# A joint between two layers: the sums of squares of the first half stand between the last down products, the other half's norm sum behind the first mixer tiles

## The reference

```python
# end of the first block
h = rmsnorm(x, g_ffn_pre) * (1 + scale_f) + shift_f
f = (silu(h @ w_gate) * (h @ w_up)) @ w_down
x = x + gate_f * rmsnorm(f, g_ffn_post)
# start of the second block
h = rmsnorm_2(x, norm_mix_w)
u = h @ w_in                     # the mixer's wide projection: z, xbc, dt and others
```

## Time and profile before

| | us |
|---|---|
| three runs: median (lowest to highest) | 1715.58 (1715.3 to 1716.63) |
| profiled execution: whole time | 1714.21 |
| profiled execution: span | 1712.4 |
| TensorE busy, share of the span | 1689.9, 99% |
| VectorE, ScalarE, GpSimd busy | 740.5, 715.5, 784.5 |

### The profile page before, as it was taken

How to read it: one execution, slowest core, us unless ns; L and a number is a source line. 1 busy time by engine, 2 the same in 40 slices (tenths; PEclk the granted TensorE clock), 3 DMA queues, 4 the chain that set the end, 5 groups by cost and what they waited for, 6 DMA issues and landing times.

```text
span 1712.4 us, 22126 instructions
## 1 busy us (share of the span) xinstructions
PE 1689.9 (99%) x8068; PEld 1373.4 (80%) x8068; DVE 740.5 (43%) x1142; ACT 715.5 (42%) x967; POOL 784.5 (46%) x612
## 2 busy tenths in 40 slices
PE   7999999999999999999999999999999999999998
PEld 5777798888888888888888888887888788888887
DVE  7767653111110046567678778675104222222002
ACT  5756454222233345334434636544223534433232
POOL 3432244444456654443443434345444444444663
PEclk9999999999999999999999999999999999999999
DMA  8655223233223323432333333223243322222332
GB/s 298 221 180 173 87 87 99 86 98 88 96 68 100 92 68 143 137 99 87 111 99 99 100 98 111 86 85 98 89 140 94 99 90 93 87 97 72 95 92 73
DMA packets 55300, 184.61 MB, mean 108 GB/s; under 512 B 5920, under 2 KB 8224, under 8 KB 54720
## 3 DMA queue, kind: packets, MB, share of 16 engines
q1 hardware_dynamic: 55232, 183.67, 33.6%
HBM read 179.39 MB, written 4.26 MB: 107 GB/s over the span
## 4 chain that ended last, share of the span: by engine, by line
PE 94%; issue 2%; DVE 2%; POOL 1%; DMA 1%; ACT 0%; SPq 0%; DVEq 0%; POOLq 0%
PE PR L560 27%; PE PR L561 26%; PE PR L564 26%; PE AX L1058 1%; PE PR L575 1%; PE PR L576 1%; PE PR L574 1%; PE AX L781 1%; PE AX L807 1%; POOL wlo L500 1%; PE AX L1062 1%; PE AX L791 1%; DMA raw<-w 1%; PE AX L597 1%; PE AX L795 1%
## 5 line engine op out<-in xcount | busy, mean ns | idle before, releaser
L500 POOL TENSOR_TENSOR wlo<-raw,whi 128x512 fp32r<-128x512 f32 (+1 forms) x600 | 778.3, 1322 | 876.4 <-ACT whi L1186 876.4
L1186 ACT ACTIVATE whi<-raw 128x1024 fp32r<-128x1024 f32 x288 | 301.5, 1051 | 141.1 <-PE PR L564 132.4
L560 PE MATMUL PR<-h3h,whi 128*128 128x512 f32 x608 | 245.5, 404 | 0.0
L561 PE MATMUL PR<-h3l,whi 128*128 128x512 f32 x608 | 240.3, 395 | 0.0
L564 PE MATMUL PR<-h3h,wlo 128*128 128x512 f32 x608 | 154.1, 395 | 0.0
L560 PE MATMUL PR<-h4h,whi 128*128 128x512 f32 x351 | 139.4, 397 | 0.0
L561 PE MATMUL PR<-h4l,whi 128*128 128x512 f32 x351 | 138.6, 395 | 0.0
L564 PEld LDWEIGHTS PR<-h3h,wlo 128*128 128x128 f32 x608 | 114.2, 188 | 27.6
L560 PEld LDWEIGHTS PR<-h3h,whi 128*128 128x128 f32 x608 | 114.3, 188 | 26.7 <-issue 1.2
L561 PEld LDWEIGHTS PR<-h3l,whi 128*128 128x128 f32 x608 | 114.4, 188 | 26.4 <-issue 1.0
L560 PE MATMUL PR<-h2h,whi 128*128 128x512 f32 x320 | 126.8, 396 | 0.1
(11 more groups left out here) (375 smaller groups left out, 2972.0 us busy)
## 6 DMA issues: line engine op xcount, KB each, us to landing
raw<-w SPq DMA_DIRECT2D x224, 512.0 KB, 3.5
cond<-wcond SPq DMA_DIRECT2D x48, 512.0 KB, 4.5
raw<-w SPq DMA_DIRECT2D x32, 384.0 KB, 3.1
raw<-w SPq DMA_DIRECT2D x32, 320.0 KB, 2.9
abc_a<-acum_rows SPq DMA_DIRECT2D x8, 512.0 KB, 4.0
abc_b<-acum_rows SPq DMA_DIRECT2D x8, 512.0 KB, 4.3
x<-xin SPq DMA_DIRECT2D x2, 1024.0 KB, 7.1
x_keep<-x SPq DMA_DIRECT2D x1, 2048.0 KB, 8.1
```

The source lines that it names most:

```text
L500: ins = pool.tensor_tensor(wlo[:, j, a:a + n], raw[:, j, a:a + n], whi[:, j, a:a + n], ALU.subtract)
L560: pe.matmul(bank, whi[:, j, w], oh[:, k0 + k, :], start=first and i == 0, stop=False)
L561: pe.matmul(bank, whi[:, j, w], ol[:, k0 + k, :], start=False, stop=False)
L1186: act.activation(whi[:, j, :], raw[:, j, :], ACT.Copy).then_inc(hi_ready, 1)
```

## The change

The sums of the squares of x for the first half (`x_sum(2)`) no longer stand behind all 44 strips. They are placed between the strips of the second half of the last down tile: after the strip given by (unit j, block k) those tiles are added that `SUMS_DN1` names, the last four before the last strip. `mix_sum(3)`, the norm sum of the down projection for the second half, goes from its place in front of the mixer into `first_units`, behind tiles 0 and 1 of the first half and ahead of the wait for tile 2. A wait for the last copy of the down results is added at the head of `first_units`. Only TensorE's list changes; ScalarE, VectorE, GpSimd and SyncE keep theirs.

```diff
+SUMS_DN1 = {(2, 1): (0,), (2, 3): (1,), (3, 1): (2,), (3, 2): (3,), (3, 3): (4, 5, 6, 7)}
...
                         mm = strip(j, fh1, fl1, k0, k, PR[:, 1 + e, :], c, j == 0 and k == 0, j == 3 and k == nk - 1)
+                        if e == 1 and (j, k) in SUMS_DN1:
+                            x_sum(2, SUMS_DN1[j, k])
                     if e == 1:
                         mm.then_inc(unit_used, 1)
                 if e == 0:
                     mm.then_inc(half_done, 1)
-            x_sum(2)
-            mix_sum(3, V_DN1 + N_DN)
...
             def first_units():
 
                 pe.wait_ge(dt_v, 1)
+                pe.wait_ge(mix_ready, R0 + N_OUT + N_DN)
                 for e, c in enumerate(HALF):
                     for k in range(KT):
+                        if e == 0 and k == 2:
+                            mix_sum(3, V_DN1 + N_DN)
                         pe.wait_ge(hh_ready, KT + KT * (2 + e) + k + 1)
```

## The result

| | before | after |
|---|---|---|
| median of nine runs (lowest to highest), us | 1715.58 (1714.54 to 1716.63) | 1719.49 (1717.25 to 1722.59) |
| ratio, 95% interval | | 1.0025 (1.0016 to 1.0033) |
| profiled execution, span | 1712.4 | 1717.7 |
| joint: first strip of the last down tile to first full-width mixer unit | 51.62 | 56.37 |

A forecast was written before the change was run, and what follows sets the result against it. TensorE, busy 99% of the span, was taken as the bound. Terms of 0.56 (first tile), 0.43 (moved sum), 1.52 (second stall), 0.15 and 0.45, taken as 3.2 on 1715.58, gave 1718.8 us; range 1716.4 to 1721.2.

The forecast's parts named there:

- One wait of 1.7 us: TensorE's wait between the last down tile's sums and the first normalised mixer tile: the change's whole target, 0.1% of the kernel.
- Sums between the strips: Last down tile on TensorE: eight moved sums cost 0.43 us each as before and find their squares ready, 0.9 to spare.
- The last down piece comes late: ScalarE ahead of the first half's Ln: square and copy of that piece come later, delaying the first mixer tile by 0.56 us.
- The other half's sum: Behind mixer tile 1: the moved norm sum adds 0.43 us, and tile 2 waits for its Ln and Exp, a 1.5 us stall.
- The two shortfalls: Tile 5's low product from GpSimd, 0.1 to 0.2 us late, and the other half's squares in the second eight sums, +0.45 us.
- Sum +3.2: Whole kernel: the added terms come to 3.1 to 3.2 us, taken as 3.2, +0.19%.
- The clock: Rival: TensorE falls to 1.2 GHz in the first stall, costing 1.6 us, +4.8 in all, 1720.4 us; chance 0.12.
- My row against it: Profile row from 30.76 to 32.24: TensorE idle for 1.48 us while its granted clock stayed at 1.00.
- likeliest case: Whole kernel: forecast of +2.5 to +3.8 us, chance 0.72, with +3.2 just inside the measurable 0.2% (3.4 us).
- The added wait: Head of the mixer's first units: waiting for the copies of all nine down pieces was to cost nothing.

The follow-up runs named there:

- e5: Changed kernel with e1's order, first half's Ln and Exp ahead of the last down piece, sums ended three strips before the tile's end: joint 51.29 us, ratio 0.9998.
- e1: Changed kernel with ScalarE's copies of tiles 2 and 3 put ahead of the other half's Ln and Exp: joint 52.68 us, ratio 1.0013.
- e2: Changed kernel with the other half's norm sum back in front of the mixer: joint 52.16 us, ratio 1.0012.
- e4: Changed kernel with the first stall filled by ten matmuls whose result nobody uses: joint 54.89 us, ratio 1.0019.
- e1b: e1 run and profiled a second time, same code on the changed kernel: joint 53.96 us, ratio 1.0009.
- a2: Changed kernel, unaltered, profiled a third time, one execution only: joint 56.36 us.
- e3: Kernel before with only the norm sum moved behind the first two mixer tiles, plus the added wait: joint 55.87 us, ratio 1.0020.
- c1: Kernel before with only the added wait for the last down piece's copy: joint 51.59 us, median 0.17 us below before.
- e6: Changed kernel with e1's ScalarE order and e4's filling of the first stall: joint 52.69 us, ratio 1.0010.
- e2b: e2 profiled a second time, same code on the changed kernel, one execution only: joint 53.67 us.
- c0: Kernel before, unaltered, timed against itself and profiled again: joint 51.68 us, median 0.65 us below before.

## Why the prediction was right, and where it was not

- **One wait of 1.7 us is all there is to win.** Nothing speaks against it: the best version, e5, got 0.33 of it.
- **Sums between the strips cost nothing and find their squares.** Held. Strips and sums took 19.50 us, 19.94 less the 0.43 of the norm sum that left; no wait among them.
- **The last down piece comes late, +0.56.** Held: 0.54 in the changed kernel, in e1 and in e2 alike, with square, copy and Ln back to back at 627.44, 627.72 and 627.98 as foretold.
- **The other half's sum, +0.43 and a stall of 1.5.** Held, slightly over-sized. From the norm sum's start to tile 2 I had 1.95; it was 1.85. With the Ln and Exp of this sum taken out from in front of tile 2 (e1), the stall went and the 0.43 stayed.
- **The two shortfalls, 0.15 and 0.45.** The right places, the first too small. The block of tile 5 took 641.63 - 639.96 = 1.67 against 1.29, +0.38; the eight sums 647.88 - 644.24 = 3.64 against 3.26, +0.38; tile 2, first behind a stall, +0.12. Together 0.89 (by the unrounded starts) instead of 0.60.
- **Sum +3.2.** Without the clock the joint grew by 3.27 (e4). The closeness is partly luck: my terms add up to 3.11 and I took 3.2, and of the terms the second stall was 0.1 too large and the shortfalls 0.3 too small.
- **The clock, +1.6, chance 0.12.** Here the step failed in its weight. Its place was right, and its price nearly (1.6 foretold; 1.47 in the changed kernel, 1.48 between it and e4). But it happened in all three profiles of the changed kernel. My row against it, an idle of 1.48 with the clock at 1.00, was weak evidence: it was shorter than the new stall by 1.2 us, and e1 and e1b show that one length of stall goes either way. At the very place of that row the idle was 1.92, 1.90 and 1.90 in three other profiles (changed kernel, a2, e3), and in all three the clock fell, 2.0 to 2.3 us behind it; here is the changed kernel:

```profile
31.75:33.67 1.92, 0.00 (x1) 0.01 (x1) 1.89 (x3) 0.00 (x0) 1.92 (x2) 1.00 0.82 262
33.67:35.90 2.23, 2.23 (x14) 2.01 (x15) 2.23 (x5) 0.39 (x1) 1.07 (x1) 1.00 0.50 167
35.90:39.31 3.41, 3.41 (x10) 2.64 (x9) 3.20 (x4) 2.17 (x4) 0.00 (x0) 0.50 0.47 160
```

In the other eleven the idle there was 1.80 or less, and the clock stayed up. So what I gave as a rival belonged in the likeliest case: +4.75 in the profiles. The medians, +3.9 and +4.0, lie inside the stated range, and at 1.0025 just beyond the 0.2% where I had put the likeliest case just inside. That they came nearer to my +3.2 than the profiled joints did is no merit of the forecast: their intervals (2.7 to 5.7 and 2.1 to 5.7) hold the joint with the fall as well as the one without it.

- **The added wait costs nothing.** Held (c1).

The rule of the Trainium skill that I had set against the change (TensorE: Matmul & The Clock Gate, Part 1: the throttled state is the default and activity releases it) pointed to this rival, and my row led me away from it. The trace agrees with that statement in this much: 3.25 us at 0.50 directly behind the 2.55 of idle, and no fall in the two profiles with the idle filled (e4, e6), where unfilled it came in four of five. Two profiles are few: they make the link likely, not certain.

## What to carry to other kernels

When one engine's work is moved, read the order of the engine that answers it: a sum finished early is worth nothing while its consumer has something later in front of it, and a sum moved late blocks everything that its consumer has queued behind it. Cost a longer stall on TensorE with the clock in it, 1.3 to 1.5 us here on top of its own length, even where a somewhat shorter stall in the same trace kept the clock. And measure an effect of a few microseconds between two landmarks around its place: here that gave 0.1 us where whole times scattered by 3.

## What the runs showed of the hardware that I had not expected

The fall of the clock is not fixed by the program. With an unbroken stall of 2.55 it fell in four of five profiles (all three of the changed kernel, one of the two of e1), with 2.00 in the one profile there was. It even fell where two matmuls broke the stall into 0.93 and 0.92, in one of two; here is the stretch from e2b's first tile on:

```profile
631.77:635.20 3.43, 3.43 (x17) 3.43 (x18) 3.00 (x8) 2.83 (x7) 1.10 (x2) 0.53 0.00 0
```

With single waits of 1.56 (three profiles), 1.14 (one) and 0.39 ahead of the first tile (two) it stayed up. What exactly decides, the runs leave open.

That two executions of one program start this stage 3.0 us apart was new to me too (607.16 before, 610.17 in c0). TensorE's first sum of squares began at 9.72 in the one and at 11.19 in the other, which is 1.47 of it. Most of the rest is the clock again. Between 30 us and the joint it fell once in the first profile of the kernel before, and twice in c0:

```profile
181.00:189.00 8.00, 7.52 (x25) 5.46 (x25) 4.13 (x8) 3.15 (x5) 2.54 (x2) 0.79 0.31 110
```

```profile
51.00:56.00 5.00, 5.00 (x27) 3.58 (x27) 2.41 (x5) 3.89 (x7) 0.00 (x0) 0.66 1.02 416
112.00:118.00 6.00, 6.00 (x21) 3.30 (x22) 4.62 (x7) 5.35 (x8) 0.48 (x1) 0.72 0.72 262
```

Each of these rows is 1.7 us of full clock missing (8.00 x 0.21, 5.00 x 0.34, 6.00 x 0.28), so one more fall and the later start come to 3.2, against the 3.0 measured. TensorE was hardly idle ahead of them (0.48 us ahead of the first, 0.57 and nothing ahead of the others); it ran matmuls of one column, 16 in the trace, shortly before each. All fourteen profiles have a fall or two between 30 and 190 us (the one at 35.90 above is such a one), with 1.7 or 3.4 us missing in all, the changed kernels and the unchanged ones alike. The seven with 1.7 reach the first landmark at 606.8 to 609.9, the seven with 3.4 at 609.6 to 610.6. From 190 us to the joint, and from the joint to 1705 us, no profile has a fall. So the falls at the joint are not the same thing happening anywhere: they come with its stalls. And a good part of the 3 us by which the first landmark scatters is falls of the clock elsewhere, in unchanged kernels too.
